# First attention: where the two halves of its output are added

## The reference

```
def one_block(qblk):
    s = jnp.einsum('bqkgd,bskd->bkgqs', qblk, k).astype(jnp.float32)
    p = jax.nn.softmax(s, axis=-1).astype(v.dtype)
    return jnp.einsum('bkgqs,bskd->bqkgd', p, v)
...
mix = jnp.concatenate([att, pool], axis=-1) @ w_out[l]
x = x + g1 * mix
```

## Time and profile before

| | |
|---|---|
| median of 3 runs | 2467.35 us |
| profiled execution | 2466.74 us |
| its span | 2465.0 us |
| busy: PE, DVE, ACT, POOL | 2343.0 (95%), 1113.7 (45%), 775.2 (31%), 863.9 (35%) |
| chain that ended last | PE 80%, DVE 9%, issue 4%, ACT 3%, POOL 2% |
| first attention | from about 200 to 425 us |
| mean granted TensorE clock | 0.985 |

### The profile page before, as it was taken

The page is one execution under the profiler, slowest core; times in us unless marked ns, Lnnn a source line. Parts: engine busy times, 40 slices in busy tenths (PEclk is TensorE's granted clock), DMA queues, the critical chain, the costliest instruction groups (busy, mean ns, idle before and its releaser), DMA issues.

```text
span 2465.0 us, 30785 instructions
## 1 busy us (share of the span) xinstructions
PE 2343.0 (95%) x11310; PEld 1924.1 (78%) x11310; DVE 1113.7 (45%) x1381; ACT 775.2 (31%) x1095; POOL 863.9 (35%) x851
## 2 busy tenths in 40 slices
PE   4997888999999999999999999999999999999997
PEld 3776777777888888888778888887778888888886
DVE  7978887479631344124463343352211122222324
ACT  3237776032310222024424454452112111212210
POOL 1445554334433333223223323332223334333331
PEclk9998999999999999999999999999999999999999
DMA  7310001524111111111131111112011111111132
GB/s 305 116 50 28 17 26 49 217 94 179 51 51 43 51 51 43 51 60 49 39 111 61 55 36 54 36 30 91 22 40 44 49 51 52 51 47 41 49 128 77
DMA packets 48318, 166.02 MB, mean 67 GB/s; under 512 B 4480, under 2 KB 6272, under 8 KB 48128
## 3 DMA queue, kind: packets, MB, share of 16 engines
q1 hardware_dynamic: 48256, 165.19, 19.3%
HBM read 156.79 MB, written 8.39 MB: 67 GB/s over the span
## 4 chain that ended last, share of the span: by engine, by line
PE 80%; DVE 9%; issue 4%; ACT 3%; POOL 2%; DMA 1%; SPq 0%; DVEq 0%; ACTq 0%; POOLq 0%
PE acc L746 62%; PE turn L971 6%; PE bank L1035 3%; DVE ADA L1655 1%; DMA WF<-in_w 1%; PE bank L1013 1%; PE acc L959 1%; PE bank L848 1%; DVE HL L1635 1%; DVE acc L1812 1%; PE turn L640 1%; ACT EX L1258 1%; PE acc L724 1%; PE bank L1110 1%; PE bank L1107 1%
## 5 line engine op out<-in xcount | busy, mean ns | idle before, releaser
L746 PE MATMUL acc<-HH,WH 128*128 128x512 f32 x1600 | 497.4, 392 | 7.3 <-POOL WL L540 6.3
L746 PE MATMUL acc<-HL,WH 128*128 128x512 f32 x1600 | 493.9, 390 | 0.0
L746 PE MATMUL acc<-HH,WL 128*128 128x512 f32 x1600 | 493.8, 390 | 0.0
L537 POOL TENSOR_TENSOR WH<-WF,CON 128x16 fp32r<-128x16 f32 x186 | 52.7, 284 | 1206.1 <-PE acc L746 1024.5
L540 POOL TENSOR_TENSOR WL<-WF,WH 128x1024 fp32r<-128x1024 f32 (+2 forms) x186 | 439.5, 2363 | 15.5
L746 PEld LDWEIGHTS acc<-HH,WH 128*128 128x128 f32 x1600 | 300.5, 188 | 74.0 <-issue 6.9
L746 PEld LDWEIGHTS acc<-HL,WH 128*128 128x128 f32 x1600 | 301.3, 188 | 62.8
L746 PEld LDWEIGHTS acc<-HH,WL 128*128 128x128 f32 x1600 | 301.1, 188 | 62.8
L538 POOL TENSOR_SCALAR WH<-WF 128x1008 fp32r<-128x1008 f32 (+2 forms) x186 | 195.4, 1050 | 0.0
L1942 DVE SCALAR_TENSOR_TENSOR CV<-EV,VEC,CV 128x1023 f32<-128x1023 f32 x44 | 99.1, 2253 | 203.9 <-ACT CV L1334 203.1
L1870 DVE SCALAR_TENSOR_TENSOR XT<-acc,MOD,XT 128x1024 f32 (+1 forms) x34 | 43.6, 1284 | 233.1 <-PE acc L746 233.1
(11 more groups left out here) (373 smaller groups left out, 4100.2 us busy)
## 6 DMA issues: line engine op xcount, KB each, us to landing
WF<-in_w SPq DMA_DIRECT2D x150, 512.0 KB, 3.4
ADA<-in_ada SPq DMA_DIRECT2D x15, 1024.0 KB, 13.1
BIAS<-in_bias SPq DMA_DIRECT2D x16, 576.0 KB, 3.8
XT<-in_xT SPq DMA_DIRECT2D x16, 512.0 KB, 10.2
ADA<-in_ada SPq DMA_DIRECT2D x4, 2048.0 KB, 11.6
ADA<-in_ada SPq DMA_DIRECT2D x3, 2560.0 KB, 9.3
WF<-in_w SPq DMA_DIRECT2D x24, 256.0 KB, 2.6
ADA<-in_ada SPq DMA_DIRECT2D x8, 512.0 KB, 3.4
```

Of the source, the lines that this page charges most:

```text
L537: pool.tensor_tensor(h[:, 0:FEW], f[:, 0:FEW], zero.to_broadcast([P, FEW]), ALU.add).then_inc(w_hi, 1)
L746: last = pe.matmul(acc[:, slot, HALF * c:HALF * c + HALF], w[slot][:, k, :], x[:, k, HALF * c:HALF * c + HALF], start=(k == 0 and w is WH ...
```

## The change

GpSimd cannot read PSUM, so ScalarE now copies both halves of the bank to SBUF: the lower one to a new tile `OTOP`, the upper one to `OTMP` as before. `gather_o` moves from VectorE's list to GpSimd's. It stands there behind the normalisation and behind `stack_queries` of slots 5, 9 and 13, and behind the loop over the slots at the round's end. Its two adds are each followed by a wait for their own semaphore. TensorE waits for the two copies (`otmp_ready`) before it overwrites the bank, no longer for the adds. One small copy on ScalarE ahead of the attention gives `otmp_ready` its first count, and VectorE's loop no longer keeps a count of its own steps.

```
+        OTOP = at("OTOP", 84, [P, HALF])
...
 (GpSimd, attend)
                    if 9 <= u <= 11 and not last:
                        stack_queries(it, 2, u - 9, it * 32 + (2 * u + 4))
+                    if u % 4 == 1 and u > 1:
+                        gather_o(it, u // 4 - 1)
                     if u == 12:
                         branch_second(it, 0)
+                gather_o(it, 3)
                 branch_second(it, 1)
+            def gather_o(it, b):
+                pool.wait_ge(otmp_ready, it * 4 + (b + 2))
+                g = b % 2
+                o = OTOP[0:64, :].rearrange("p (i j q) -> p i j q", j=2, q=P)
+                m = OTMP[0:64, :].rearrange("p (i j q) -> p i j q", j=2, q=P)
+                if g == 0:
+                    pool.wait_ge(ml_ready, it * 2 + (b // 2 + 1))
+                pool.tensor_tensor(OT[0:64, 2 * g:2 * g + 2, :], o[:, :, 0, :], m[:, :, 0, :], ALU.add).then_inc(o_first, 1)
+                pool.wait_ge(o_first, it * 4 + (b + 1))
+                pool.tensor_tensor(OT[64:128, 2 * g:2 * g + 2, :], o[:, :, 1, :], m[:, :, 1, :], ALU.add).then_inc(o_ready, 1)
+                pool.wait_ge(o_ready, it * 4 + (b + 2))
 (TensorE, values)
-                        pe.wait_ge(o_ready, it * 4 + (b + 1))
+                        pe.wait_ge(otmp_ready, it * 4 + (b + 1))
 (ScalarE, other_parts and ahead of the attention)
                 act.wait_ge(o_ready, it * 4 + (b + 1))
+                act.activation(OTOP[0:64, :], bank6[0:64, :], ACT.Copy)
                 act.activation(OTMP[0:64, :], bank6[64:128, :], ACT.Copy).then_inc(otmp_ready, 1)
+            act.activation(SUM[:, 2:3], eps, ACT.Copy).then_inc(otmp_ready, 1)
 (VectorE: gather_o is gone, and its two calls)
-            with steps.loop(3, 4) as it:
+            with dve.Fori(0, 3) as it:
```

More of the change, by code:

```diff
@@ L303, in build @@
             sem("mh_ready"), sem("ml_ready"))
-        gated, gh_ready = sem("gated"), sem("gh_ready")
+        o_first, gated, gh_ready = sem("o_first"), sem("gated"), sem("gh_ready")
         silu_done = sem("silu_done")
@@ L1818, in invert_sums @@
                 dve.reciprocal(RC[:, j:j + 1], SUM[:, j:j + 1]).then_inc(rc_ready, 1)
[L1820 to L1829, removed]
             def attend(it, last):
@@ L1836, in attend @@
                         largest(it, u + 2)
-                    if u % 4 == 1 and u > 1:
-                        gather_o(it, u // 4 - 1)
                     for h in range(2):
@@ L1848, in attend @@
                         modulation(ADA3[j][:, :], C1B, MOD1[:, block_of(it * 2 + (16 + j))])
-                gather_o(it, 3)
             dve.wait_ge(cond_ready, 4)
```

## The result

The changed kernel takes 2480.46 us (median of 5 runs, 2477.02 to 2481.16). The kernel before, in the same measurement, takes 2469.02 (5 runs, 2466.99 to 2470.51). The ratio is 1.004, with a 95% interval from 1.0029 to 1.005: slower by 11.4 us. The forecast was 2473.4, or +6.1. The sign is right; the size is not, and the time lies outside the range of 2467.5 to 2478. Of the 7.1 us between forecast and result, 1.7 belong to the base: the three runs shown had a median of 2467.35, and with five it is 2469.02 (in the later measurements 2469.5 to 2470.5).

A forecast was written before the change was run, and what follows sets the result against it. No engine was full: VectorE paces plain slots, GpSimd slots 9 to 11, one chain the round ends. Rounds 0 to 2 +7.0, round 3 -1.1, prologue +0.2 give +6.1 on 2467.35: 2473.4 us, range 2467.5 to 2478.

The forecast's parts named there:

- 1.55 fits in it. Cost 0: End of round 3: the +1.55 us delay fits in TensorE's 2.48 us wait for output-projection weights, so cost 0.
- one addition on GpSimd: Each 64x256 add on GpSimd takes 0.75 us, against 0.41 on VectorE.
- additions to normalisation, slot 9: GpSimd in slot 9: two adds with their semaphore waits take 1.81 us ahead of the normalisation for slot 11.
- slot 5, gain per round: Slot 5, rounds 0 to 2: VectorE starts PTL earlier and GpSimd gathers in idle time, -0.51 us.
- slot 9 to 13, per round: Rounds 0 to 2: gather behind QL delays slot 11's normalisation, and slot 13 has the second copy; +1.3 us.
- slot 13 to the round's end, per round: Rounds 0 to 2: slot 13's delay is passed on to the round's last values, with 0 further change.
- round's end, per end: Between rounds: extra copy and GpSimd's adds lengthen the chain from copy to MH, uncovered, +1.55 us each.
- round 3, its three gatherings: Last round, slots 5, 9 and 13: GpSimd is free without QL, gains about 0.42, 0.25 and 0.42, -1.1 us.
- prologue, the added copy: Ahead of the attention: a one-column ScalarE copy at the head of the starting chain, +0.2 us.
- attention, without the prologue: All four rounds: 7.0 us for rounds 0 to 2 and -1.1 for round 3, +5.9 us.
- rival (c): Slower: VectorE product collides with GpSimd in slot 13, and TensorE's clock falls after round-end gaps; 2478 us, chance 0.14.

The follow-up runs named there:

- Experiment 7: Kernel before, with two or four extra 0.6 us ScalarE copies ahead of the last round's last OTMP copy: 2471.0 us (+1.4) and 2472.07 us (+2.5).
- experiment 9: Changed kernel, fourth output-projection ADA load issued behind the third pair's first weights: 2476.72 us; also with fourth gatherings on VectorE and additions ahead of stacking: 2469.64 us.
- experiments 8: Changed kernel with only the very last of its sixteen gatherings back on VectorE: 2478.38 us, +8.8 against the kernel before.
- experiment 5: Kernel before with both halves copied by ScalarE and TensorE waiting for the copies only, additions still on VectorE: 2474.73 us, +5.2.

## Why the prediction was wrong

The step that failed is the last one, on the end of round 3: "1.55 fits in it. Cost 0". I let TensorE's 2.48 us wait for weights take the delay up and looked no further. It does take up much of TensorE's own delay, though not all: the wait itself was 2.48 us in the profile I had and 1.42 and 1.19 in the two later ones of the same kernel, whose TensorE was slower through the lower clock. And VectorE's products, which follow TensorE, come later against loads whose start is set by the last values. In the changed kernel that start is followed by a gap of 4.99 us where there were 3.64, and the low clock behind it adds to the delay. The products slid far enough onto the split for the fourth to wait for the subtraction, and the ADA load and the weights behind it went out 3.4 us late. Measured: 99.39, 101.70 and 99.59 us in place of 97.64, 97.59 and 97.50, so +2.65. Experiment 7 makes it in the kernel before, experiment 9 takes it out of the changed one. All this is read from output projections in single executions; how often the phase falls so in the unprofiled runs is not shown. I had the pair of rows that shows such a collision, in the very stage, and looked for it in slot 13 alone, where it did not come (1.21 us for the product in round 1).

Point by point, averages over five profiles with the attention of either kernel (for the changed one, its three and those of experiments 8 and 9):

| term | forecast | measured |
|---|---|---|
| one addition on GpSimd | 0.75 | 0.73 |
| additions to normalisation, slot 9 | 1.81 | 1.70 |
| slot 5, gain per round | -0.51 | -0.65 |
| slot 9 to 13, per round | +1.3 | +1.46, with the low clock +2.3; mean +1.96 |
| slot 13 to the round's end, per round | 0 | -0.15 |
| round's end, per end | +1.55 | +1.53 (19.68 against 18.15) |
| round 3, its three gatherings | -1.1 | -1.6 |
| second QH to the first slot 5 | 0 | -0.13 |
| prologue, the added copy, start to start with QH | +0.2 | +0.1 |
| attention, without the prologue | +5.9 | +6.3 (217.96 against 211.64) |
| last round's end | 0 | +2.65 |

The attention came out as forecast, in part by luck: the low clock in slot 11, which I did not price (the wait there I did), is set off by gains that I put too small. The +1.53 at a round's end is luck in part too. At the first two ends the way takes 18.86 us in the changed kernel and 17.61 in the kernel before where the clock stays high, so the chain itself costs 1.25, less than my 1.55, and the low clock makes up the rest. There rival (c) was half right: the low clock is behind every end, 15 of 15, but the kernel before has it behind 12 of 15, so it adds only some 0.3 to the difference. Against the one profile that I had, with 17.62 and 17.72 us, it would have added 0.5 per end.

6.3 and 2.65 make 9.0 of the 11.2 to 11.4 us. The other 2 us stay open. The stretch from there to GpSimd's split at 708.2 us in the first profile of before, and to the same split in the others, took 188.3, 189.8 and 190.1 in the kernel before and 192.8, 190.7 and 189.7 in the changed one, and three profiles of each don't tell that from chance. What follows took 1756.2 to 1756.8 in the former and 1752.2 to 1756.7 in the latter.

## What to carry to other kernels

A delay that "fits into" a wait shifts everything else that runs beside that wait: before it is put at zero, list what other engines and queues do in the next stage, and which of them start from another event. An idle stretch of TensorE costs its length and then some, so price it from several profiles: one execution can be the lucky one. And an addition moved to an engine that looks idle is free only at a place in the order where that engine is idle: the change cost slots 9 to 13 1.5 to 2.3 us with the two instructions behind the subtraction and 0.45 with them ahead of it, and experiment 5 shows the same 0.45 with the second copy and no addition on GpSimd.

## What the runs showed of the hardware

TensorE's clock went to 1.2 GHz for some microseconds after waits as short as 2.3 us (9 of 15 in slot 11, five profiles), in the wait or behind it. It did not do so in any round of the one profile with 36 and 14 small transpositions in the gaps. Two executions of the kernel before differ by 2.3 us in the attention of 212 us, 2.2 of it in the three ways to slot 5, where the low clock lies.

A VectorE product with both inputs in SBUF takes 1.22 us alone, 2.04 when it starts during GpSimd's one-input split and 3.40 when it starts during its two-input subtraction. GpSimd pays as well: 2.00 for 1.04, and 3.24 for 2.36. The lengths add up as turns of whole instructions: each is its own length and what was left of the other engine's. So a small shift of phase decides whether a product waits for the long one (here between distances of 0.90 and 1.14).

GpSimd's two-input addition of 64x256 in fp32 takes 0.73 us, by the same 2.10 ns per element and 0.2 us fixed as its subtractions of 512 and 1024; VectorE's takes 0.42, from SBUF as from the bank.
